# A hybrid S5 / stick-breaking attention step: a later exponential of the seventh block, and the new tokens' inputs as one block-diagonal product

## What is computed

```python
proj = rmsnorm(x) @ w_in                      # 2048 -> 10240 columns
u_a, z_a, q, k, v, z_b, g_a, g_b = split(proj)
# S5: 64 groups of 16 channels, 64 complex states each
a_bar = exp(lam * dt); b_bar = ((a_bar - 1) / lam) * B
h[t] = a_bar * h[t - 1] + b_bar @ u[t]        # new tokens: h = a_bar * h0 + b_bar @ u
y_a = gelu(real(C @ h) + D * u); y_a = y_a * sigmoid(y_a @ glu_w + glu_b) * silu(z_a)
# attention, per head and block of 128 queries
z = q @ k.T * scale + bias; log_keep = where(valid, -softplus(z), 0)
later = reverse_cumsum(log_keep) - log_keep
w = where(valid, exp(log_sigmoid(z) + later), 0); o = (w @ v) * silu(z_b)
merged = sigmoid(g_a) * (y_a @ w_branch_a) + sigmoid(g_b) * (o @ w_branch_b)
out = rmsnorm(x + merged @ w_out)
```

## Time and profile before

| | |
|---|---|
| median of 3 runs | 3023.15 us (3022.87 to 3023.61) |
| profiled execution | 3023.83 us, span 3022.0 us |
| mean granted TensorE clock | 0.995 |
| busy share of the span | PE 98%, PEld 96%, DVE 45%, ACT 34%, POOL 14% |
| PE instructions | 19132 matmuls |
| chain that ended last | PE 87%, DVE 4%, POOL 3%, DMA 2% |

### The profile page before, as it was taken

The page is one execution under the profiler, slowest core; times in us unless marked ns, Lnnn a source line. Parts: engine busy times, 40 slices in busy tenths (PEclk is TensorE's granted clock), DMA queues, the critical chain, the costliest instruction groups (busy, mean ns, idle before and its releaser), DMA issues.

```text
span 3022.0 us, 48554 instructions
## 1 busy us (share of the span) xinstructions
PE 2968.9 (98%) x19132; PEld 2907.7 (96%) x19132; DVE 1345.6 (45%) x2563; ACT 1014.5 (34%) x1210; POOL 433.2 (14%) x1118
## 2 busy tenths in 40 slices
PE   6999999999999999999999999999999999999998
PEld 5999999999999999999999999999999999999997
DVE  6624443462444345244434524443557544422266
ACT  5135215413521541352154135216421421221142
POOL 7400330240033023003203300420000000000000
PEclk9999999999999999999999999999999999999999
DMA  6331333233232223313322332332348754332283
GB/s 182 81 105 61 89 81 99 73 83 107 66 91 78 89 73 91 102 64 92 90 90 59 94 99 64 92 105 75 134 146 284 254 183 154 95 122 69 78 247 115
DMA packets 425714, 329.03 MB, mean 109 GB/s; under 512 B 64738, under 2 KB 387890, under 8 KB 423474
## 3 DMA queue, kind: packets, MB, share of 16 engines
q1 hardware_dynamic: 425522, 326.34, 36.1%
HBM read 235.72 MB, written 73.73 MB: 102 GB/s over the span
## 4 chain that ended last, share of the span: by engine, by line
PE 87%; DVE 4%; POOL 3%; DMA 2%; issue 2%; ACT 1%; SPq 1%; POOLq 0%; DVEq 0%; ACTq 0%
PE acc L1811 78%; PE side L1778 3%; PE side L1952 2%; DMA t_sig_ga<-work 1%; PE side L1947 1%; POOL prologue L1164 1%; DVE work L1535 1%; PE side L1905 0%; PE side L1906 0%; PE side L2067 0%; DMA work<-work 0%; ACT w_high L912 0%; DVE work L1542 0%; DMA w_raw<-in_w_branch_a 0%; SPq L509 0%
## 5 line engine op out<-in xcount | busy, mean ns | idle before, releaser
L1811 PE MATMUL acc<-x_high,w_high 128*128 128x344 f32 (+2 forms) x5440 | 1220.4, 327 | 4.4 <-DVE x_low L1395 2.0
L1811 PE MATMUL acc<-x_low,w_high 128*128 128x344 f32 (+2 forms) x5440 | 1180.3, 320 | 0.0
L1811 PE MATMUL acc<-x_high,w_low 128*128 128x344 f32 (+2 forms) x5440 | 1176.5, 319 | 0.0
L1811 PEld LDWEIGHTS acc<-x_high,w_high 128*128 128x128 f32 x5440 | 908.9, 188 | 23.4 <-issue 13.2
L1811 PEld LDWEIGHTS acc<-x_low,w_high 128*128 128x128 f32 x5440 | 921.4, 189 | 0.0
L1811 PEld LDWEIGHTS acc<-x_high,w_low 128*128 128x128 f32 x5440 | 912.4, 188 | 0.0
L1380 DVE TENSOR_TENSOR w_low<-w_raw,w_high 128x1024 fp32r<-128x1024 f32 x233 | 287.7, 1235 | 604.2 <-ACT w_high L912 601.5
L912 ACT CAST w_high<-w_raw 128x1024 fp32r<-128x1024 f32 x232 | 242.2, 1044 | 891.6 <-PE acc L1811 794.1
L1257 POOL COPY work<-s_tables 128x28 f32 x16 | 3.3, 208 | 1499.9 <-DVE work L1528 1235.6
L1528 DVE TENSOR_TENSOR work<-work,side 128x128 f32<-128x128 f32 x64 | 18.4, 287 | 318.5 <-PE side L1952 318.5
L1778 PE MATMUL side<-work 128*128 128x128 f32 (+5 forms) x704 | 129.4, 312 | 1.1 <-POOL work L1276 1.1
(11 more groups left out here) (303 smaller groups left out, 2361.4 us busy)
## 6 DMA issues: line engine op xcount, KB each, us to landing
w_raw<-in_w_in SPq DMA_DIRECT2D x160, 512.0 KB, 3.9
w_raw<-in_w_out SPq DMA_DIRECT2D x48, 512.0 KB, 3.9
work<-t_sig_ga SPq DMA_DIRECT2D x24, 516.0 KB, 4.6
out<-work SPq DMA_DIRECT2D x18, 512.0 KB
t_qk<-stage SPq DMA_DIRECT2D x16, 516.0 KB, 5.0
work<-t_qk SPq DMA_DIRECT2D x16, 516.0 KB, 4.9
t_sig_gb<-stage SPq DMA_DIRECT2D x16, 516.0 KB, 4.2
t_sig_ga<-stage SPq DMA_DIRECT2D x16, 516.0 KB, 4.2
```

Source lines behind the costliest of these rows:

```text
L1811: ins = mm(acc[s][:, a, 0:n], w[b][:, kk, :], x[:, kx, c0:c0 + n], start=start, stop=stop)
```

## The change

- `us_diag`, a tile of [128, 2, 32] set to zero once by POOL in the prologue, replaces `Us`. Its block g (partitions 32 g to 32 g + 15, columns 8 g to 8 g + 7) gets the inputs of group g, with four DMAs in place of one. The count of `ug_in` goes from 144 to 192.
- At BT, ACT also copies the first 32 columns of each group of `M1` to `B0`. At KM, PE also transposes `B0`, and ACT copies the transpose to `B0T`. At YM one matmul `B0T` x `us_diag` of 32 columns replaces the four of 8 columns.
- At KM the four matmuls use all 128 columns of `M1` as weights in place of the first 16, so that they write 128 partitions. ACT and DVE wait for the copy `B0` before they write over `M1`.
- The exponential of the weights of the seventh block is issued on ACT at step 72 (`EXP`) in place of 71, behind `split_hi` and GA0's evacuation there. DVE's part stays at 71.
- In the last pass ACT rounds the first tile of `y_a` at step 72, behind that exponential; the second goes from 74 to 75 on ACT and DVE.

```diff
@@ -136,6 +136,8 @@
     newsum = sb("new_squares", [P, 8])
     newvar, rstd1, w1 = sb("new_variance", [P, 1]), sb("new_rstd", [P, 1]), sb("new_newton", [P, 1])
     zero1 = sb("zero1", [P, 1])
+    us_diag = sb("u_new_diagonal", [P, 2, HG * NEW])
+    B0 = sb("first_inputs", [P, P])[:, :]
     pages = sb("pages", [1, NEW * N_PAGES], I32)
     acc = [nc.alloc_psum_tensor(f"acc{s}", [P, NB, 512], F32) for s in range(2)]
     side = nc.alloc_psum_tensor("side", [P, 2, 512], F32)
@@ -205,13 +207,13 @@
     SO = c.take(P, HG * NEW)
     Bc, Bm = c.take(HG * GC), c.take(HG * GC)
     BcX, BmX = Bc.rearrange("p (g c) -> p g c", g=HG), Bm.rearrange("p (g c) -> p g c", g=HG)
-    Us = c.take(8 * NEW, GC).rearrange("p (g b) -> p g b", g=8)
     h12 = c.take(2 * HG * NEW).rearrange("p (f g b) -> p f g b", f=2, g=HG)
     hA = c.take(HG * NEW).rearrange("p (g b) -> p g b", g=HG)
     hn_flat = c.take(HG * NEW)
     hn = hn_flat.rearrange("p (g b) -> p g b", g=HG)
     ysT = c.take(P, NEW)
     fo = c.take(P, HG)
+    B0T = c.take(P)
     c.at = WORK - (12 * HG + 6 * HG + NEW)
     pw = c.take(12 * HG)
     turn = c.take(6 * HG).rearrange("p (a g) -> p a g", a=6)
@@ -290,6 +292,7 @@
     u_ready = sem("u_ready")
     s5_in, seed_in, seed_ready, s_seed_ready, seed_out, m_ready, n_ready, n_in, ha_ready = [sem(s) for s in
         ("s5_in", "seed_in", "seed_ready", "state_seed_ready", "seed_out", "s5_m_ready", "s5_n_ready", "s5_n_in", "s5_ha_ready")]
+    b0_ready, b0_mm, b0t_ready = sem("s5_b0_ready"), sem("s5_b0_mm"), sem("s5_b0t_ready")
     b_mm, bt_ready, k_mm, kt_ready, kt_pad, toep_in = [sem(s) for s in
         ("s5_b_mm", "s5_bt_ready", "s5_k_mm", "s5_kt_ready", "s5_kt_pad", "s5_toep_in")]
     u_sent, ug_in, yj_sent, yj_in, pq_mm, v_ready, y_mm, yj_ready, fin_ready, p_copied, t_ready, swap_in = [sem(s) for s in
@@ -487,7 +490,9 @@
                 rows = t_u.rearrange("(g c) (t j) -> t c g j", c=GC, t=CH)
                 for tau in range(CH):
                     sp.dma_start(Ug[tau * GC:(tau + 1) * GC], rows[CH - 1 - tau][:, :, 0:NCH]).then_inc(ug_in, 16)
-                sp.dma_start(Us, t_us.rearrange("(g c) b -> c g b", c=GC)).then_inc(ug_in, 16)
+                us_rows = t_us.rearrange("(f g c) b -> g c f b", f=2, g=HG)
+                for g in range(HG):
+                    sp.dma_start(us_diag[g * 2 * GC:g * 2 * GC + GC, :, g * NEW:(g + 1) * NEW], us_rows[g]).then_inc(ug_in, 16)
 
             def y_rows(hf):
 
@@ -815,7 +820,8 @@
     ST = (48, 51, 55, 59, 63, 67, 71, 75)
     WT = (51, 54, 58, 62, 66, 70, 74, 78)
     PV = tuple(p + 1 for p in WT)
-    Y_AT = (74, 74, 75, 76, 76, 77, 79, 79)
+    EXP = (48, 51, 55, 59, 63, 67, 72, 75)
+    Y_AT = (74, 75, 75, 76, 76, 77, 79, 79)
 
     @block.scalar
     def _(act):
@@ -925,7 +931,7 @@
                 if p == (76 if last else 72):
                     evacuate(i, GA0, last)
                 if last:
-                    for t in range(FT):
+                    for t in range(1, FT):
                         if p == Y_AT[t]:
                             y_high(t)
                 if p == ZB_AT:
@@ -934,9 +940,13 @@
                     if p == BT[hf]:
                         act.wait_ge(b_mm, 2 * i + hf + 1)
                         nc.scalar.copy(B1T, side[:, 0, :].rearrange("p (g s) -> p g s", g=HG)).then_inc(bt_ready, 1)
+                        nc.scalar.copy(B0.rearrange("p (g c) -> p g c", g=HG), M1[:, :, 0:2 * GC]).then_inc(b0_ready, 1)
                     if p == KM[hf]:
                         act.wait_ge(k_mm, 2 * i + hf + 1)
+                        act.wait_ge(b0_ready, 2 * i + hf + 1)
                         nc.scalar.copy(Kt[:, :, 7 * GC:15 * GC], side[0:GC, 0, :].rearrange("p (g q) -> p g q", g=HG)).then_inc(kt_ready, 1)
+                        act.wait_ge(b0_mm, 2 * i + hf + 1)
+                        nc.scalar.copy(B0T, side[:, 1, 0:P]).then_inc(b0t_ready, 1)
                     if p == YM[hf]:
                         act.wait_ge(y_mm, 2 * i + hf + 1)
                         act.wait_ge(st_sent, i * 320 + 160 * hf + PRIMED)
@@ -959,12 +969,14 @@
                     nc.scalar.copy(smp, side[0:NEW, 0, 0:3 * P]).then_inc(new_ready, 1)
                 for qb in range(8):
                     w = P * (qb + 1)
-                    if p == ST[qb]:
+                    if p == EXP[qb]:
                         act.wait_ge(arg_ready, 8 * i + qb + 1 + PRIMED)
                         nc.scalar.activation(zb[qb % 2][:, 0:w], zb[qb % 2][:, 0:w], ACT.Exp).then_inc(w_ready, 1)
                     if p == WT[qb]:
                         act.wait_ge(w_tr, 8 * i + qb + 1)
                         nc.scalar.copy(wT[:, 0:w], side_flat[:, 0:w]).then_inc(wt_ready, 1)
+                if last and p == EXP[6]:
+                    y_high(0)
                 for qb in range(8):
                     w = P * (qb + 1)
                     if p == SC[qb]:
@@ -1140,6 +1152,7 @@
         nc.gpsimd.memset(zero1[:, :], 0.0).then_inc(pool_chain, 1)
         nc.gpsimd.memset(ident[:, :], 0.0).then_inc(pool_chain, 1)
         nc.gpsimd.memset(cmask[:, :], 0.0).then_inc(pool_chain, 1)
+        nc.gpsimd.memset(us_diag[:, :, :], 0.0)
         nc.gpsimd.memset(ones, 1.0)
         pool.wait_ge(pool_chain, 3)
         nc.gpsimd.affine_select(out=ident[:, :], in_=ident[:, :], compare_op=ALU.not_equal, fill=1.0, base=0,
@@ -1481,6 +1494,7 @@
                         turning(i, hf, ch, range(5, 7))
                     if p == KM[hf]:
                         dve.wait_ge(k_mm, 2 * i + hf + 1)
+                        dve.wait_ge(b0_ready, 2 * i + hf + 1)
                         V.memset(Kt[:, :, 0:7 * GC], 0.0).then_inc(kt_pad, 1)
                     if p == PQ[hf]:
                         dve.wait_ge(pq_mm, 2 * i + hf + 1)
@@ -1887,28 +1901,28 @@
                         pe.wait_ge(n_ready, 2 * i + hf + 1)
                         pe.wait_ge(bt_ready, 2 * i + hf + 1)
                         for g in range(HG):
-                            last_op = one(side[0:GC, 0, g * P:(g + 1) * P], M1[:, g, 0:GC], N1[:, g, 0:CH * GC])
+                            last_op = one(side[:, 0, g * P:(g + 1) * P], M1[:, g, :], N1[:, g, 0:CH * GC])
                         last_op.then_inc(k_mm, 1)
+                        pe.wait_ge(b0_ready, 2 * i + hf + 1)
+                        tr(side[:, 1, 0:P], B0, ident[:, :]).then_inc(b0_mm, 1)
                     if p == PQ[hf]:
 
                         pe.wait_ge(kt_ready, 2 * i + hf + 1)
                         if hf == 0:
-                            pe.wait_ge(ug_in, i * 144 + 144)
+                            pe.wait_ge(ug_in, i * 192 + 192)
                         for g in range(HG):
                             last_op = one(side[:, 0, g * P:(g + 1) * P], B1T[:, g, :], Ug[:, HG * hf + g, :])
                         last_op.then_inc(pq_mm, 1)
                     if p == YM[hf]:
                         pe.wait_ge(v_ready, 2 * i + hf + 1)
+                        pe.wait_ge(b0t_ready, 2 * i + hf + 1)
                         pe.wait_ge(toep_in, (i * 2 + (hf + 1)) * (16 * CH))
                         for g in range(HG):
                             out = side[:, 0, g * P:(g + 1) * P]
                             mm(out, Toep[:, g, :], Ug[:, HG * hf + g, :], start=True, stop=False)
                             mm(out, N1[:, g, GC:9 * GC], V1[:, g, 0:NCH], start=False, stop=True)
                         tr(side[0:HG, 1, 0:P], V1[:, :, NCH], ident[:, :])
-                        for g in range(HG):
-                            a = 256 + g * NEW
-                            last_op = one(side[:, 1, a:a + NEW], B1T[0:GC, g, :], Us[:, HG * hf + g, :])
-                        last_op.then_inc(y_mm, 1)
+                        one(side[:, 1, 256:256 + HG * NEW], B0T, us_diag[:, hf, :]).then_inc(y_mm, 1)
                     if p == YS[hf]:
                         pe.wait_ge(hn_ready, 2 * i + hf + 1)
                         pe.wait_ge(yj_ready, 2 * i + hf + 1)
```

## The result

| | before | after |
|---|---|---|
| median (lowest to highest) of 6 runs | 3023.01 us (3022.70 to 3023.61) | 3005.99 us (3003.53 to 3013.49) |
| ratio, 95% interval | | 0.9948 (0.9938 to 0.9959) |
| profiled execution, span | 3023.83, 3022.0 | 3007.13, 3005.3 |
| busy share: PE, DVE, ACT, POOL | 98, 45, 34, 14% | 98, 45, 34, 14% |
| PE instructions | 19132 matmuls | 19052 matmuls |

The change brings 17.0 us of the 25.5 forecast. The time misses the range that the prediction gives for its own mechanism, 2995.5 to 3001. It lies inside the wider one, 2994 to 3006.5, by 0.5 us, and only because that was stretched to take in rival C, which did not come: that it holds is luck.

The account below looks back on a forecast made before the run. TensorE (PE) was taken to bound the kernel; 15.7 + 2.6 - 1.4 + 4.8 + 3.8 = 25.5 us off 3023.83 gives 2998.3, and a median of 2997.6. Own range 2995.5 to 3001, wider range 2994 to 3006.5.

Parts of the forecast that it names:

- rival C: PV stalls stay, exponential or copy being late behind GA0's sigmoid; 8.6 us of gain missing, 3006.2; chance 0.10.
- Step 1: YM on PE, 16 times: fewer records and no narrow-shape surcharge, 2.11 for 3.09; gain 0.98 each, 15.7 us.
- Step 2: KM on PE, 16 times: full matmuls plus a transpose, 1.00 for 1.16; gain 0.16 each, 2.6 us.
- Rival A: At YM and KM the new forms pay the surcharge too; gain 8.9 in place of 18.3, 3007.0; chance 0.07.
- Step 3: ACT's two new copies per half, and the waits for B0 before writing over M1, cost 0.
- Steps 5 and 6: Seventh block's exponential moved: PV stalls go, 4.8 us in 7 looped passes; last pass's casts moved too: 3.8 us.
- Step 4: POOL's second half: PE comes sooner than N1 allows in some passes; loss 1.4 us, bounds 0 and 2.9.
- Its own sign of being wrong: Many PE waits for POOL's last instruction (L1276) or DVE's scan (L1509) would prove the prediction wrong.
- the slack of 0.70: Second half: N1 is ready at 671.70, PE's KM starts at 672.40, so POOL has 0.70 us to spare.
- Step 7: SP issues three more DMAs per pass, 1.3 us (to 2.7) before the Toeplitz DMAs; cost taken as 0.
- rival D: Toeplitz DMAs and DVE's scan late behind SP's new issues, YM of first halves waits; slower, up to 3033; chance 0.03.
- Rival B: SP's three issues push POOL's second-half parameters by 1.3 us; loss 13.4 in place of 1.4, 3009.6; chance 0.08.

Follow-up runs that it names:

- e11: On e5, four full matmuls of 8 columns at YM in place of the one of 32 columns; 3003.63 us, ratio 0.9943 to the kernel before.
- e8: Changed kernel with KM's four matmuls back at 16 weight columns; 3006.39 us, ratio 0.9955 to the kernel before.
- e1: Kernel before with only the seventh block's exponential and the last pass's first two tile casts moved; 3013.29 against 3021.78 us, ratio 0.9972.
- e5: Changed kernel with POOL's second-half parameter loads (six DMAs) issued by ACT at step 13 in place of SP; 2995.09 against 3021.02 us, ratio 0.9915.
- e4: Changed kernel with the four diagonal loads issued later on SP, between the two swaps of chunk 4, with their own semaphore; 3006.68 us, ratio 0.9951.
- e6: Changed kernel with the four loads of us_diag issued by ACT at step 9, SP keeping POOL's parameters; 3005.40 us, ratio 0.9950 to the kernel before.
- e3: Kernel before with only its load of Us cut into four DMAs on SP; 3022.15 against 3021.78 us, ratio 1.0003.

## Why the prediction was right in direction and wrong in size

**Step 1, YM: right.** 0.98 forecast; measured 3.09 - 2.13 = 0.96 and, in first halves, 3.07 - 2.11 = 0.96. Both of its parts stand, the records and the surcharge (e11), and the weight loads have no gap in front of the new matmul, where a gap of 0.2 was to prove the step wrong. In all 16 bursts YM takes 16.6 less, where 15.7 was forecast; 2.3 of the 16.6 are pass 0's first YM, which waits for DVE. That one burst costs between 4.0 and 7.5 us in the kernels run here, with and without the change, so nothing is made of it.

**Step 2, KM: right by itself.** 0.17 measured, 0.16 forecast. Rival A (the surcharge isn't that of narrow shapes) falls with e8 and e11. The Trainium skill, TensorE: Matmul & The Clock Gate, LDWEIGHTS, by which only columns count, gives no gain from more rows; the 0.29 between the narrow form and e11 was such a gain, so the measurement decides there. The drain of TensorEngine Tiling (Array Packing), Key Properties, in the same skill agrees with it in sign, as with the 0.24 of KM.

**Step 3: right.** No wait for the copies to `B0` or `B0T` shows.

**Steps 5 and 6: right.** The eight PV bursts of the seventh block cost 12.4 against 21.4, 9.0 less, and the eighth block's in the last pass 0.2 more (the forecast left 0.4 there): 8.8 against 4.8 + 3.8 = 8.6, and 8.5 measured in e1. ACT's exponential starts at 556.61 and the copy is over before PE wants it. DVE's idle 1.96 is gone: the subtraction follows its neighbour at once.

```profile
555.48 1.09 DVE L1550 TENSOR_TENSOR work<-work 128x896 f32<-128x896 f32 x1
556.49 1.22 DVE L1393 TENSOR_TENSOR w_low<-w_raw,w_high 128x1024 fp32r<-128x1024 f32 x1
```

Rival C falls.

**Step 4, POOL: this is the step that failed.** It took 1.4, with 2.9 as the bound, and 11.3 - 1.2 = 10.1 was lost. The prediction counted the passes in which the landing *had* ended POOL's wait (3) and let POOL move along with `y_mm` in the others. It never asked when the parameters land there. Its own sign of being wrong, many waits for POOL's last instruction, is what came: eight, where it expected two or three. POOL starts at the later of the two. In the kernel before, `y_mm` let it start 3.27 us behind YM's start. The parameters were there 2.0 to 3.1 us behind it in passes 2 to 7 (issue to landing of SP's last load in each), and since POOL starts 0.16 behind a landing that it waits for, they were hidden by 0.05 to 1.1. With YM shorter, `y_mm` alone would let POOL start at 2.43 (so in e5), and that is sooner than four of these six landings allow. Pass i = 2 of the kernel after, in the timeline of POOL:

```profile
642.09 0.21 POOL L1270 COPY work<-s_tables 128x28 f32 x1 [33.08 <-DMA work<-t_state_seeds]
```

```profile
667.78 0.38 POOL L1289 TENSOR_TENSOR work<-work 128x64 f32<-128x64 f32 x1
```

YM starts at 638.71 there, so POOL starts 3.38 behind it, later than the 3.27 of before. In e5 the same pass has

```profile
635.24 0.21 POOL L1276 COPY work<-s_tables 128x28 f32 x1 [32.12 <-PE side L1798]
```

with YM at 632.81, 2.43 behind.

The upper bound of 2.9 held the landings and POOL's work where they were. By the landings and the work of each pass of the kernel before, N1 would be late by 1.6, 2.2, 0.3 and 0.1 us in passes 0, 1, 5 and 7: an estimate of some 4.1, or 2.9 more than the 1.2 of before. So the uncovered landing alone gives no more than the bound. The rest of the 10.1 is that in the kernel after the landings come later still and POOL's work takes longer. The starts show it, as means over passes 2 to 7 or 1 to 7:

- PE's KM of the second half is due 28.61 behind YM's start, where it started at 29.68: 1.07 sooner. With the slack of 0.70 that makes 0.37, near the bound's 0.28.
- POOL does not stand still, it gets later: N1 is ready 29.70 behind YM's start, where it was at 28.98. Some 0.2 of these 0.7 are the start, and 0.5 is the work, which takes 26.2 in place of 25.7. In pass 1 of the kernel before, where the landing starts POOL too, it was 26.2 as well.
- PE's burst costs 1.25 more, 0.16 beyond the 1.09 by which N1 is late.

The passes without a stall show that start and work count together. In pass 5 of e4 the parameters landed 2.28 behind YM's start, POOL started at 2.44, and KM was on time. In passes 1 and 5 of e6 and 2 and 5 of e8 the landing started POOL as well, at 2.6 to 3.2; but its work took only 25.2 to 25.7, and KM was on time again. So a landing behind `y_mm` alone does not make the stall; what lengthens the work is argued further down. What e5 shows is that moving the landing away removes both, the later start and the longer work.

**Step 7, SP: right in its result, not in all of its reason.** The loads of the new tokens' inputs take 0.423 each, and one of them 1.68:

```profile
L495 SPq DMA_DIRECT2D u_new_diagonal<-t_u_new x32: 423/423/1679, 88.7 to 1920.0; - x32
```

In pass i = 2 the four took 3.10 where the one took 0.43, and the Toeplitz DMAs behind them went out later. SP's timeline after:

```profile
615.68 3.10 SPq L495 DMA_DIRECT2D u_new_diagonal<-t_u_new  x4
619.04 0.41 SPq L374 DMA_DIRECT2D w_raw<-in_w_in  x1
619.63 4.58 SPq L514 DMA_DIRECT2D work<-work  x7
```

L514 starts 638.71 - 619.63 = 19.1 ahead of YM, where it was 20.1. In the seven passes 1 to 7 such a push is there twice (1.0 and 0.5). PE doesn't feel it at YM: the wait for DVE's scan is there once, as before, so rival D falls. Rival B named a price close to the one found (13.4 in place of 1.4, against 11.3), and its 3009.6 is nearer to the 3005.99 than the forecast is. That is luck, since its cause is not the one found: e3 has the issues without the price, e4 and e6 most of the price without the issues.

**What stays open.** In the kernel after, the parameters land 0.5 us later relative to YM than before (3.3 against 2.8, mean of passes 1 to 7). The three issues don't explain it: in e3 it is 3.0, in e4 and e6 3.3. Single issues of SP that take 0.4 to 1.3 us longer, at places that shift from pass to pass, can be seen in all kernels. One other part can be read from the traces. SP's swap in front of DVE's scan (L519, L520) lands 2.3 to 2.4 us after the issue of its second DMA in most passes; in passes 3 and 6 of the kernel after it takes 3.5, the scan and SP's second swap come 1.2 later, and the parameters wait behind that swap in SP's queue. All eight kernels with the single matmul at YM have 3.0 to 3.7 us in just these two passes, with and without the new loads on SP; the kernel before, e1 and e3 have 3.4 to 3.5 in pass 5 instead (the first also 3.0 in pass 7). Why these passes isn't settled, and there is one profiled execution of each kernel. The profiled execution of after also has 2.4 us in pass 0 for DVE's low part (L1393, 3.7 us in all). Kernels with and without the change show between none (e11) and 3.7 us for this wait, with 3.4 in e3, so it is put down to no part of the change.

A second load came uncovered, which no step of the prediction has: the two bursts that transpose V (L1939) in passes 1 and 7 cost 1.0 more, since PE waits there for V's load. In the nine kernels with the diagonal product PE loses 0.3 to 1.5 us so; in the four without it these bursts never cost over 0.02 more.

The sum by measured terms: 16.6 (YM) + 2.7 (KM's form) - 10.1 (POOL) + 9.0 - 0.2 (PV) - 2.4 (KM of pass 0) - 1.0 (V) = 14.6. The spans differ by 16.7; the 2.1 between lie outside these bursts and were not followed.

## What to carry to other kernels

When an engine waits for two things, the view of waits names the later one only. Before making that one earlier, read in every pass when the other one arrives, since the gain can end there: here the landing was hidden behind `y_mm` by 0.05 to 1.1 us in passes 2 to 7, and 0.96 taken from PE at YM came back as 1.25 lost at the next meeting. A load that two engines need in time should be issued by whichever queue is free when its buffer is, not by the one that has always issued it: the move of six DMAs from SP to ACT was worth some 11 us after the change and 3.2 before it, so the order of a queue has to be looked at again after each change of what it feeds.

## What the runs showed of the hardware

- With 128 weight columns, small float32 matmuls go by the number of their records: eight of 8 columns take 0.82 us (e11), eight of 128 columns 0.89. Joining four into one matmul pays there, giving each fewer moving columns hardly does. It is no rule for all small matmuls: at YS, with 8 weight columns and 16 moving, eight records take 440.61 - 440.32 = 0.29 us until the transpose starts (kernel after):

```profile
440.32 0.36 PE L1792 MATMUL side<-work 128*8 128x16 f32 x8
440.61 0.28 PE L1931 MATMUL side<-ident,work 128*32 128x128 f32 x1
```

- Narrow shapes cost 0.24 (16 weight columns, KM) and 0.29 us (16 rows, YM) a burst on top.
- A stall costs PE more than the wait of its matmuls: 9.1 us of those were 11.3 for the weight loads, and 11.3 us of time. In e6 it was 6.2, 7.6 and 7.5.
- The same POOL program took from 25.2 to 26.6 us in the second halves of these kernels. Its operations of 128 x 64 last longer beside some of DVE's. In pass i = 2 of the kernel after three of the last five instructions took 0.47, beside DVE's operations of 256 elements:

```profile
665.88 0.47 POOL L1280 TENSOR_TENSOR work<-work 128x64 f32<-128x64 f32 x1
666.31 0.47 POOL L1281 TENSOR_TENSOR work<-work 128x64 f32<-128x64 f32 x1
```

```profile
666.12 0.94 DVE L1467 TENSOR_TENSOR work<-work 128x256 f32<-128x256 f32 x2
```

In e5, where POOL is 0.95 us earlier in the pass, they run beside operations of 4 elements:

```profile
659.47 0.29 POOL L1287 TENSOR_TENSOR work<-work 128x64 f32<-128x64 f32 x1
659.72 0.29 POOL L1288 TENSOR_TENSOR work<-work 128x64 f32<-128x64 f32 x1
```

```profile
659.56 0.29 DVE L1479 TENSOR_TENSOR work<-work 128x4 f32<-128x4 f32 x2
```

The Trainium skill, GPSIMD Engine Reference, Specifications, says that GpSimd shares its ways to SBUF with VectorE and contends with its instructions that read two inputs there. The trace agrees with that, 0.47 against 0.29, and so do all thirteen traces together: behind the prologue, 738 of POOL's TENSOR_TENSOR operations of this shape overlap a TENSOR_TENSOR of DVE's with 128 columns or more, and 353 of them took over 0.40 us; none of the other 4257 did. But no run here moved DVE's work alone, so as a cause it is argued, not shown.
